# The opening of the first expert is multiplied for all 256 tokens between the steps of the routing, and turned through a one-hot matrix

## The reference, cut to what matters

```python
N_EXPERTS, TOP_K, D_FF = 8, 2, 3584
def swiglu(x, w_gate, w_up, w_down):
    return (jax.nn.silu(x @ w_gate) * (x @ w_up)) @ w_down

def moe_ffn(x, router_w, w_gate, w_up, w_down):
    logits = (x @ router_w).astype(F32)
    top_val, top_idx = lax.top_k(logits, TOP_K)
    gates = jax.nn.softmax(top_val, axis=-1)
    combine = jnp.sum(jax.nn.one_hot(top_idx, N_EXPERTS) * gates[..., None], axis=-2)
    for e in range(N_EXPERTS):
        out = out + combine[..., e:e + 1] * swiglu(x, w_gate[e], w_up[e], w_down[e])
    return out
```

## Time and profile before

| | |
|---|---|
| median of 3 runs | 1687.88 us (1685.31 to 1690.2) |
| the profiled execution | 1689.82 us, its span 1688.0 us, 1.8 us lie around the span |
| PE busy | 1571.5 us, 93% of the span |
| DVE, ACT, POOL busy | 1273.0, 920.9, 162.8 us |
| layer 1 normalised, block 0 (end of line 1025) | 655.33 us |
| first matmul of OPENING, expert 0 | 692.59 us |
| first matmul of the loop of ROUNDs | 709.36 us |
| last matmul | 1655.4 us |

### The profile page before, as it was taken

The page is one execution under the profiler, slowest core; times in us unless marked ns, Lnnn a source line. Parts: engine busy times, 40 slices in busy tenths (PEclk is TensorE's granted clock), DMA queues, the critical chain, the costliest instruction groups (busy, mean ns, idle before and its releaser), DMA issues.

```text
span 1688.0 us, 22489 instructions
## 1 busy us (share of the span) xinstructions
PE 1571.5 (93%) x8642; PEld 1267.0 (75%) x8642; DVE 1273.0 (75%) x1136; ACT 920.9 (55%) x761; POOL 162.8 (10%) x177
## 2 busy tenths in 40 slices
PE   8888999999898797599999999999999999999991
PEld 7657478888776574488888888888888888888881
DVE  7985655444529756388888888888888888888883
ACT  1144133434204331377777777777777777777770
POOL 0342085000004400200000000000000000000000
PEclk9989999999999998799999999999999999999996
DMA  8693165554433202699999999999999999999962
GB/s 311 247 314 137 52 218 205 198 176 152 171 133 118 76 3 100 237 363 374 355 395 391 355 394 370 375 395 348 398 394 349 395 395 350 396 389 366 393 254 89
DMA packets 192882, 469.57 MB, mean 278 GB/s; under 512 B 7024, under 2 KB 11248, under 8 KB 192304
## 3 DMA queue, kind: packets, MB, share of 16 engines
q1 hardware_dynamic: 189360, 453.70, 73.3%
q0 software_dynamic: 2304, 10.77, 1.6%
q10 hardware_dynamic: 1152, 4.19, 0.6%
HBM read 461.29 MB, written 25.17 MB: 288 GB/s over the span
## 4 chain that ended last, share of the span: by engine, by line
issue 59%; PE 28%; DVE 10%; DMA 1%; ACT 1%; POOL 1%; POOLq 0%; SPq 0%; DVEq 0%
PE ps L1429 9%; PE ps L1402 4%; PE ps L1440 4%; PE ps L1755 2%; DVE arena L960 2%; PE ps L1409 1%; PE ps L1693 1%; DVE arena L993 1%; PE ps L1707 1%; PE ps L1703 1%; DVE arena L977 1%; DVE small L1013 1%; DMA arena<-in_w_in 0%; DVE x L1021 0%; DVE x L1025 0%
## 5 line engine op out<-in xcount | busy, mean ns | idle before, releaser
L1036 DVE TENSOR_TENSOR lo<-arena,hi 128x2048 fp32r<-128x2048 f32 x378 | 868.4, 2302 | 222.5 <-ACT hi L641 221.9
L641 ACT ACTIVATE hi<-arena 128x2048 fp32r<-128x2048 f32 x378 | 723.3, 1919 | 356.8 <-PE ps L1429 229.8
L1429 PE MATMUL ps<-hi,xg 128*128 128x512 f32 x1792 | 556.0, 392 | 3.2 <-DVE xg L1042 2.6
L1429 PEld LDWEIGHTS ps<-hi,xg 128*128 128x128 f32 x1792 | 336.7, 189 | 75.9 <-DVE lo L1036 3.4
L1429 PE MATMUL ps<-lo,xg 128*128 128x512 f32 x896 | 350.1, 391 | 0.0
L1440 PE MATMUL ps<-hi,hTe 128*128 128x512 f32 x896 | 283.8, 398 | 2.2 <-DVE hTe L1066 2.2
L1429 PEld LDWEIGHTS ps<-lo,xg 128*128 128x128 f32 x896 | 169.0, 189 | 35.5
L1440 PEld LDWEIGHTS ps<-hi,hTe 128*128 128x128 f32 x896 | 164.8, 189 | 35.0 <-DVE lo L1036 2.6
L1440 PE MATMUL ps<-lo,hTe 128*128 128x512 f32 x448 | 175.8, 392 | 0.0
L1429 PE MATMUL ps<-hi,xs 128*128 128x512 f32 x448 | 140.1, 394 | 2.9 <-issue 2.9
L1402 PE MATMUL ps<-arena 128*128 128x256 f32 x544 | 126.2, 395 | 3.4 <-DMA arena<-in_w_in 2.2
(11 more groups left out here) (329 smaller groups left out, 1371.5 us busy)
## 6 DMA issues: line engine op xcount, KB each, us to landing
arena<-in_mg SPq DMA_DIRECT2D x112, 1024.0 KB, 7.0
arena<-in_mu SPq DMA_DIRECT2D x112, 1024.0 KB, 6.9
arena<-in_md SPq DMA_DIRECT2D x112, 1024.0 KB, 7.0
arena<-in_w_in SPq DMA_DIRECT2D x7, 2048.0 KB, 11.2
arena<-in_wg SPq DMA_DIRECT2D x14, 1024.0 KB, 5.1
arena<-in_wu SPq DMA_DIRECT2D x14, 1024.0 KB, 5.1
arena<-in_wd SPq DMA_DIRECT2D x14, 1024.0 KB, 4.9
xg_rows<-in_zeros SPq DMA_DIRECT2D x1, 8704.0 KB, 35.2
```

The lines of the kernel that those rows point to most:

```text
L641: af(hi[r % PARTS][:, :], raw[r % RAWS], ACT.Copy).then_inc(hi_ready, 1)
L1036: tt(lo[r % PARTS][:, :], raw[r % RAWS], hi[r % PARTS][:, :].bitcast(F32), ALU.subtract)\
L1429: ins = mm(ps[:, (4 if w == "G" else 4 + nb) + b, :], tok[a][:, kk * nt + b * P:kk * nt + (b + 1) * P], tiles_of(part[r % PARTS], w)[:, k, ...
```

## The change

Layer 1 now also splits the turned x into `xs`, as layer 0 does, and the opening of expert 0 (pieces 0 to 3) is multiplied with both blocks of `xs`: 96 matmuls instead of 48. They are put between the steps of the routing in PE's list: piece 0 with block 0 before block 1 is turned; piece 1 with block 0 between the router products and the five counting products; the other 72 after the counting products and before `tokens_turned`. ACT and DVE get the splits of pieces 3 to 6 and the silu and product for 128x1024 numbers (256 tokens) at fixed places in their lists. DVE makes `pick`, for each block a 128x128 matrix with a one where the token of the partition has the rank of the column in expert 0 (four operations after the row numbers). Instead of four transposes of `hh` against the identity, eight matmuls of `hh` against `pick` (four tiles, two blocks) both turn and pick the rows. `experts(0)` then begins with the ROUND; the second pass, `experts(NE)`, keeps its OPENING. `xg_in` lies elsewhere, as `xs` is now in use. The copies into `xT` are regrouped, three on ACT and one on DVE, each 128x512.

The core of the diff (the places where only names or banks follow are left out):

```diff
-        xg_in = arena[:, A_XS:A_XS + D]
+        xg_in = arena[:, A_HT + 3072:A_HT + 3072 + D]
+        pick = score_rows[:, 2 * D:2 * D + T].rearrange("p (b s) -> p b s", b=2)
...
             def experts(first):
-                expert(first, OPENING, 0, True)
+                if first:
+                    expert(first, OPENING, 0, True)
...
# ACT
+                def row_copy(q):
+                    b, k = q // 2, q % 2 * 4
+                    act.wait_ge(xt_psum, 12 + q + 1)
+                    af(xT[:, k:k + 4, b * P:(b + 1) * P], by_block(q, 1), ACT.Copy).then_inc(xt_act, 1)
+                for q in range(4):
+                    b, k = q // 2, q % 2 * 4
+                    if q % 2 == 0:
+                        norm(2 * l, (b,))
+                    if l and q < 3:
+                        row_copy(q)
+                    elif l:
+                        act.wait_ge(xt_dve, 5)
+                    act.wait_ge(xt_psum, 4 * (n_x + 1) + q + 1)
+                    af(xs_x[0][:, k:k + 4, b * P:(b + 1) * P], by_block(q, l), ACT.Copy).then_inc(xs_hi, 1)
...
             af(rt[:, 100:102], rt[:, 98:100], ACT.Exp).then_inc(gate_exp, 1)
+            high_part(0, PARTS)
+            act.wait_ge(piece_used, NP + 2)
+            af(sg[:, :], ps[:, 4:6, :].rearrange("p a n -> p (a n)"), ACT.Silu).then_inc(gate_silu, 1)
+            high_part(0, PARTS + 1)
+            high_part(0, PARTS + 2)
             tokens_high(1)
+            high_part(0, PARTS + 3)
+            act.wait_ge(ht_psum, FC + 1)
+            af(hT_e[turned_in(0)][0][:, :], ps[:, 6, :], ACT.Copy).then_inc(ht_hi, 1)
             experts(0)
...
# DVE
                 norm(2 * l, (0, 1, 2, 5), lambda q: dve.wait_ge(res_psum, 4 * l + q + 1),
-                     (lambda: xs_low(0)) if l == 0 else None)
+                     lambda: xs_low(0))
+                if l:
+                    dve.wait_ge(xt_psum, 16)
+                    v_.tensor_copy(xT[:, 4:8, P:T], by_block(3, 1)).then_inc(xt_dve, 1)
+                xs_low(1)
...
+            for b in range(NB):
+                step.then(ts(pick[:, b, :], C("iota"), r1[:, b:b + 1], None, ALU.is_equal))
+                ins = stt(pick[:, b, :], C("iota"), r2[:, b:b + 1], pick[:, b, :], ALU.is_equal, ALU.add)
...
+            low_part(0, PARTS)
             most = dve.value_load(count_i[0:1, 0:1], min_val=0, max_val=T)
+            low_part(0, PARTS + 1)
+            dve.wait_ge(piece_used, NP + 4)
+            dve.wait_ge(gate_silu, FC + 1)
+            tt(hh[:, :], ps[:, 6:8, :].rearrange("p a n -> p (a n)"), sg[:, :], ALU.mult).then_inc(h_ready, 1)
+            low_part(0, PARTS + 2)
             tokens_low(1)
+            low_part(0, PARTS + 3)
+            dve.wait_ge(ht_hi, FC + 1)
+            tt(hT_e[turned_in(0)][1][:, :], ps[:, 6, :], hT_e[turned_in(0)][0][:, :].bitcast(F32), ALU.subtract)
...
# PE
+            def first_inward(r, b):
+                pe.wait_ge(lo_ready, NP + r + 1)
+                pe.wait_ge(xs_lo, 4 + 2 * (b + 1))
+                return inward(*SEQ[r], r, b, NB, xs, T)
+            transpose_x(3, None, (0,))
+            first_inward(0, 0)
+            transpose_x(3, None, (1,))
+            pe.wait_ge(xs_lo, 4 + 2)
             for b in range(NB):
-                transpose_x(3, (4, 3, 6, 7), (b,))
-                pe.wait_ge(xt_act, (8, 10)[b])
+                pe.wait_ge(xt_act, (6, 7)[b])
                 if b:
-                    pe.wait_ge(xt_dve, 6)
+                    pe.wait_ge(xt_dve, 5)
                 for k in range(KT):
                     ins = mm(ps[:, 0, NE * b:NE * (b + 1)], xT[:, k, b * P:(b + 1) * P], rw[:, k, :],
             ins.then_inc(lg_psum, 1)
+            first_inward(1, 0)
             pe.wait_ge(sel_ready, 1)
...
+            first_inward(0, 1).then_inc(piece_used, 1)
+            first_inward(1, 1).then_inc(piece_used, 1)
+            for r in (2, 3):
+                first_inward(r, 0)
+                first_inward(r, 1).then_inc(piece_used, 1)
             tokens_turned(None, 16)
+            pe.wait_ge(h_ready, FC + 1)
+            pe.wait_ge(pick_ready, 1)
+            for q in range(4):
+                for b in range(NB):
+                    ins = mm(ps[:, 6, q * P:(q + 1) * P], hh[:, 512 * b + q * P:512 * b + (q + 1) * P], pick[:, b, :],
+                             start=(b == 0), stop=(b == 1))
+            ins.then_inc(ht_psum, 1)
+            pe.wait_ge(xg_hi, 1)
+            pe.wait_ge(xg_lo, 1)
             experts(0)
```

More of the change, by code:

```diff
@@ L337, in at, with by_block @@
             return n if i is None else i * each + (each + n)
-        def by_block(q):
-            return ps[:, (4, 3, 0, 1)[q], :].rearrange("p (k t) -> p k t", k=4)
+        def by_block(q, l=0):
+            return ps[:, q if l else (4, 3, 0, 1)[q], :].rearrange("p (k t) -> p k t", k=4)
         AFTER_H = [AT["G", 1, 0]] + [AT["D", j - 1, 0] for j in range(1, FC)]
@@ L831, in norm @@
                             .then_inc(ln_std, 1)
[L833 to L841, removed]
+                def row_copy(q):
[12 more added lines that the diff above has]
+                    af(xs_x[0][:, k:k + 4, b * P:(b + 1) * P], by_block(q, l), ACT.Copy).then_inc(xs_hi, 1)
+                if l == 0:
                     channel_mixer()
                     norm(1)
[L844 to L849, removed]
             act.wait_ge(gate_exp_in, 1)
             af(rt[:, 100:102], rt[:, 98:100], ACT.Exp).then_inc(gate_exp, 1)
+            high_part(0, PARTS)
[3 more added lines that the diff above has]
+            high_part(0, PARTS + 2)
             tokens_high(1)
+            high_part(0, PARTS + 3)
+            act.wait_ge(ht_psum, FC + 1)
+            af(hT_e[turned_in(0)][0][:, :], ps[:, 6, :], ACT.Copy).then_inc(ht_hi, 1)
             experts(0)
@@ L1301, in _ @@
                          dve.wait_ge(piece_used, NP))
-            for q in range(2, 4):
-                dve.wait_ge(xt_psum, 16 + q + 1)
-                v_.tensor_copy(xT[:, 2 * q:2 * q + 2, P:T],
-                               ps[:, (4, 3, 6, 7)[q], :].rearrange("p (k t) -> p k t", k=2)[:, :, P:T])\
-                    .then_inc(xt_dve, 1)
             def r8(a, n=16):
@@ L1349, in _ @@
             ts(row_of[:, 2:4], m2, float(P * NE), None, ALU.add).then_inc(rows_ready, 1)
+            r1, r2 = rt[:, 110:112], rt[:, 112:114]
+            step(ts(r1, m1, float(P * NE), None, ALU.add))
+            step.then(ts(r2, m2, float(P * NE), None, ALU.add))
+            for b in range(NB):
+                step.then(ts(pick[:, b, :], C("iota"), r1[:, b:b + 1], None, ALU.is_equal))
+                ins = stt(pick[:, b, :], C("iota"), r2[:, b:b + 1], pick[:, b, :], ALU.is_equal, ALU.add)
+                if b:
+                    ins.then_inc(pick_ready, 1)
+                else:
+                    step(ins)
             step.wait()
@@ L1386, in transpose_x @@
                     for k in range(KT):
-                        if n == 1:
-                            dst = by_block(2 * b + k // 4)[:, k % 4, :]
+                        if n in (1, 3):
+                            dst = by_block(2 * b + k // 4, n // 3)[:, k % 4, :]
                         else:
@@ L1392, in transpose_x @@
                         ins = tr(dst, x[:, b, k * P:(k + 1) * P], ident)
-                        if k % 4 == 3 if n == 1 else (b or n == 3) and k % 2:
+                        if k % 4 == 3 if n in (1, 3) else b and k % 2:
                             ins.then_inc(xt_psum, 1)
```

10 lines of the change are left out of this document (6 added, 4 removed).

## The result

The changed kernel takes 1671.95 us in the median of 4 runs (1667.57 to 1673.9), beside 1686.9 us (1685.31 to 1690.2) for the kernel before in the same comparison. The ratio is 0.9905, with a 95% interval of 0.988 to 0.9931: 15 us faster, beyond the noise of the measurement. The forecast was 1678.0 in a range from 1672.5 to 1684.5.

A forecast was written before the change was run, and what follows sets the result against it. TensorE bounds the loop, so its start sets the end. Routing +3.2 (ranks 677.7), the 72 matmuls to 694.5, then 5.0: loop at 699.5, not 709.36, 9.9 us gained; 1687.88 - 9.9 = 1678.0, range 1672.5 to 1684.5.

The forecast's parts named there:

- The loop is bound by TensorE and its start sets the end: Expert loop: TensorE busy 120.90 of 121.00 us per expert, length fixed; its start, 709.36, sets the end.
- rival 2: Expert loop: weights become the bound and give the gain back, 1687.9 or some 3 us more; 5%.
- rivals 3 and 4: 3: lower clock through the 72 matmuls, 1692, 4%. 4: late waits break up the 72, within 0.3% of now, 3%.
- Piece 0 with block 0: 5.12 us: Layer 1, before block 1 is turned: twelve matmuls almost wholly at the lower clock, 659.39 to 664.5.
- Turning and router products: +2.5: Turning block 1 and router products: logits 4.2 later at lower clock, 0.3 to 1.2 earlier at upper; took +2.5.
- Piece 1 and the counting products: +0.7: Between router and counting products: twelve matmuls hidden or costing 2.3, took +1.2; counting products give back 0.5.
- The 72 and what follows them: After the counting products: 72 matmuls 16.3 us plus 0.5, end 694.5; then 5.0 us, mostly VectorE, to the loop.
- slack of 2.7 us: Token rows, 13.6 us after the ranks, land 2.7 us before TensorE comes to turn them.
- Nothing behind it changes: From the loop's start on: the 9.9 us gained there stays as it is to the end.
- The low bound of the range: Best case: routing -2.3, then 16.3 and 5.0, loop at 693.5, 15.9 us gained; range from 1672.5.

The follow-up runs named there:

- tokens_first: Changed kernel with VectorE's split of the token rows put ahead of the split of piece 5; 1671.51 us, ratio 0.9904.
- skip24: Changed kernel without the 24 matmuls of block 1 with pieces 2 and 3; 1671.11 us.
- plus24: Changed kernel with 24 more matmuls, result unread, behind the 72 and ahead of turning the token rows; 1677.05 us, ratio 0.9927.
- first_burst_only: Changed kernel with the 12 matmuls of piece 1 with block 0 moved behind the counting products; 1673.89 us, ratio 0.9922.
- after: The changed kernel itself, first comparison; median 1671.95 us, ratio 0.9905, profiled run 1671.07 us.
- bursts_behind: Changed kernel with the 24 early matmuls (pieces 0 and 1 with block 0) moved behind the counting products; 1681.01 us, ratio 0.9964.
- before_filled: Kernel before the change, with matmuls whose result nobody reads put into TensorE's waits, nothing moved; 1684.06 us, ratio 0.9978.
- bursts_filled: bursts_behind with 12 matmuls, result unread, at each of the two places where the early matmuls had stood; 1678.21 us, ratio 0.9944.
- skip24_thin3: skip24 with VectorE's split of piece 3 also cut to 8 of its 2048 columns; 1670.66 us.
- tokens_first_filled: tokens_first with 12 matmuls, result unread, in TensorE's gap before the first burst (piece 0 with block 0); 1673.19 us, ratio 0.9916.
- after_third: Changed kernel run again unaltered, for a third profile; 1669.28 us in a single run.
- after_again: Changed kernel run again unaltered, for a second profile; 1672.29 us, ratio 0.991.

## Why the prediction was off

- *The loop is bound by TensorE and its start sets the end.* Right. An expert is unchanged, the weights did not hold it up (rival 2 fell: TensorE gained at the loop's start and kept it), and rivals 3 and 4 didn't come about.
- *Piece 0 with block 0: 5.12 us.* Wrong, 2.86. I took layer 0's course in one execution as the course of layer 1; in two of the three executions of the changed kernel layer 0 does not have that course itself. (The 0.59 of the window 218 to 219 puts the turn at 218.8, not 218.6, which changes nothing here.) Its start was right (659.39 forecast from a block that was normal at 655.33; 659.68 from 655.58), its clock was not. In three profiles of the changed kernel the clock did not fall in the gap at all, in five of its variants it fell and was back within the burst. Four of these five (tokens_first, skip24, plus24, first_burst_only) differ from the changed kernel only behind the gap, so what decides about the gap, worth 1.3 to 1.4 us at the logits, is open.
- *Turning and router products: +2.5.* This is the step that failed. The logits came 2.5 us earlier than before and not 2.5 later. Of these 5.0 us, 2.2 are the twelve above and 2.8 the turning and the router products, which took 4.57 us from the end of the twelve where I had 7.35. I gave the lower and the upper clock even odds and then leaned to the lower. The runs showed that the odds for the router products were not even: in all ten profiles with an early burst or twelve filled matmuls before both router blocks (after three times, and the seven variants below it in the table other than bursts_behind and before_filled) the router products had 1.00. In bursts_behind, where the bursts are gone from there, they had 0.50. The burst that I booked as a price is what has the clock up for what follows it, whether or not it fell in the gap before.
- *Piece 1 and the counting products: +0.7.* Measured 5.45 us from logits to ranks, against 5.11 before: +0.3. The size was right. Here the clock did fall, inside the burst (0.59 in 668 to 669 us and 0.50 in 669 to 671 in the profiled run).
- *The 72 and what follows them.* 16.3 and 5.2 us, against 16.8 and 5.0. Right. The slack of 2.7 us was right without a collision (2.6), but VectorE's split held a scatter and left 1.0 of it, which cost nothing here. The Trainium skill (SBUF — State Buffer, Who interferes with whom) says that a tensor_tensor with both inputs in SBUF contends with GpSimd's reads, but infers that it does not stall DMAs issued by GpSimd. The runs here speak against that inference for an indirect DMA: the operation that held the scatter 2 us is a subtraction with two SBUF inputs, and cutting it gave the 2 us back. Which of the scatter's accesses was held is not tested.
- *Nothing behind it changes.* Wrong by 3.2 us in the profile. The loop before started out of a wait of 3.3 us for VectorE's product (705.67 to 708.95, then the turning) and spent a stretch at 0.50 right after it; the changed loop does not (10.0 of 10.0 us busy at 1.00 in 695 to 705). That part, 1.6 us, is tied to the gap: filling it in before_filled took it away. The other 1.6 us is a stretch at 0.50 near the last expert's end, in both profiles of before and in none of the three of after; but it stands in five variants of the changed kernel too (bursts_behind, bursts_filled, skip24_thin3, tokens_first, tokens_first_filled), and what decides it is open.

So the mechanism of the gain was right, and the clock was mis-sized, by 5.0 us at the logits and, in the profiles, by 3.2 inside the loop. The low bound of the range took the upper clock for the routing, and so had the logits at most 1.2 us earlier than before; it had the twelve start at the lower clock, and the high clock at the loop's start had no place in it.

## What to carry to other kernels

Real work that is moved into the waits of TensorE can pay twice when what follows is a chain of small products: once as work, and once because the small products then run at the upper clock. Here, by the medians, it was 5.9 us of the one and 2.8 of the other. Matmuls without use in the same kind of wait paid where they kept or brought the clock up for what followed; in before_filled twelve of them ran at the lower clock and stood in the way. When two ways are put beside each other, count the slack again with the operations that now overlap for the first time; a scatter issued on GpSimd lost 2 us to a VectorE subtraction that used to run at another time.

## What the runs showed of the hardware

- The router's 32 matmul records with 8 columns each take 3.64 us at 1.00 and 6.83 (bursts_behind) at 0.50, a ratio of 1.88, nearly that of the clock, though they hardly stream any columns.
- In the profiled run of the changed kernel the clock outlived the last dense matmul of the burst (ending at 662.6) through 1.0 us of transposes and 3.6 us of router products, and fell at about 668.
- Behind an idle wait of 2.9 us in layer 0 and the same burst, the clock differed between executions of one kernel: 1.00 throughout in after_third and after_again, 0.50 in 216 to 220 us in after.
- The length of the loop took one of three values in the fourteen profiles: 942.8, 944.4 or 946.0 us, by none, one or two stretches at 0.50 at its start or end.
- An indirect DMA issued by GpSimd keeps it busy for 0.95 to 1.09 us, and for 2.95 to 3.07 when it begins inside a VectorE split (128x2048, two SBUF inputs), in eight profiles. In the other direction GpSimd's scaling stretched such a split from 2.29 to 5.34 us (skip24).
